# A two-layer streaming encoder step: Toeplitz steps by row halves, a reordered head, q swaps ahead of splits, attention weights in halves

## What is computed

```python
mod = c @ w_ada[layer] + b_ada[layer]                 # the "ada" product
h = rms_norm(x, norm_g[layer]) * (1.0 + scale) + shift
q, k, v, g_a, u, g_s = jnp.split(h @ w_in_even[e], EVEN_SPLITS, axis=-1)
q, k = rope(q), rope(k)
m = jnp.maximum(jnp.max(s, axis=-1, keepdims=True), sink)
p = jnp.exp(s - m)
p = p / (jnp.sum(p, axis=-1, keepdims=True) + jnp.exp(sink - m))
```

## Time and profile before

| what | value |
| --- | --- |
| median of 3 runs | 2287.86 us (2286.92 to 2289.37) |
| the profiled execution's own time | 2290.1 us |
| its span | 2288.3 us |
| mean granted TensorE clock | 0.949 of full |
| TensorE busy | 94% |
| VectorE, ScalarE, GpSimd busy | 36%, 22%, 20% |
| data moved by DMA | 414.93 MB, 181 GB/s on average |

### The profile page before, as it was taken

The page is one execution under the profiler, slowest core; times in us unless marked ns, Lnnn a source line. Parts: engine busy times, 40 slices in busy tenths (PEclk is TensorE's granted clock), DMA queues, the critical chain, the costliest instruction groups (busy, mean ns, idle before and its releaser), DMA issues.

```text
span 2288.3 us, 26857 instructions
## 1 busy us (share of the span) xinstructions
PE 2153.8 (94%) x10930; PEld 1674.9 (73%) x10946; DVE 815.9 (36%) x1506; ACT 498.9 (22%) x1030; POOL 451.8 (20%) x319
## 2 busy tenths in 40 slices
PE   8886899899999999999999999999998989999996
PEld 2356666688887767888887578887886757788885
DVE  7444262433335543122434522114152442422222
ACT  1132343322321421001214311002112431200010
POOL 0033514455524001101123010101023001100011
PEclk9887999899999999999999999999878989999998
DMA  8876744688787425554585245554733313344431
GB/s 279 286 203 230 261 151 173 233 306 295 253 291 245 163 86 177 214 185 166 187 268 172 82 166 212 192 184 155 214 114 108 110 37 111 113 146 148 147 131 59
DMA packets 86271, 414.93 MB, mean 181 GB/s; under 512 B 12404, under 2 KB 13460, under 8 KB 51892
## 3 DMA queue, kind: packets, MB, share of 16 engines
q1 hardware_dynamic: 79360, 396.37, 49.5%
q10 hardware_dynamic: 6788, 16.84, 2.6%
HBM read 323.51 MB, written 86.33 MB: 179 GB/s over the span
## 4 chain that ended last, share of the span: by engine, by line
PE 88%; DVE 4%; DMA 2%; issue 1%; POOL 1%; ACT 1%; SPq 0%; DVEq 0%; ACTq 0%; POOLq 0%
PE bank L699 21%; PE bank L700 21%; PE bank L701 21%; PE bank L954 5%; PE bank L644 3%; PE bank L720 2%; PE bank L719 2%; PE bank L913 1%; PE bank L832 1%; PE bank L914 1%; PE bank L790 1%; PE bank L894 1%; PE bank L820 1%; PE bank L763 1%; DMA parts_scratch<-pair 1%
## 5 line engine op out<-in xcount | busy, mean ns | idle before, releaser
L699 PE MATMUL bank<-p_hh,pair 128*128 128x512 f32 x1952 | 785.3, 402 | 28.0 <-POOL pair L464 14.7
L700 PE MATMUL bank<-p_hl,pair 128*128 128x512 f32 x1952 | 775.9, 398 | 0.0
L701 PE MATMUL bank<-p_hh,pair 128*128 128x512 f32 x1952 | 773.1, 396 | 0.0
L699 PEld LDWEIGHTS bank<-p_hh,pair 128*128 128x128 f32 x1952 | 372.9, 191 | 128.3 <-POOL pair L464 16.1
L701 PEld LDWEIGHTS bank<-p_hh,pair 128*128 128x128 f32 x1952 | 372.5, 191 | 83.0
L700 PEld LDWEIGHTS bank<-p_hl,pair 128*128 128x128 f32 x1952 | 373.0, 191 | 80.1 <-issue 1.4
L464 POOL TENSOR_TENSOR pair<-ring,pair 128x1024 fp32r<-128x1024 f32 x62 | 154.8, 2500 | 194.0 <-ACT pair L455 194.0
L1289 POOL TENSOR_TENSOR pp_mem<-pp_mem 128x512 f32<-128x512 f32 x48 | 62.1, 1294 | 619.2 <-ACT pp_mem L1054 619.2
L1378 POOL TENSOR_TENSOR p_g<-p_t,pp_mem 128x512 f32<-128x512 f32 x32 | 41.3, 1290 | 577.3 <-DVE p_t L1834 577.3
L1708 DVE SCALAR_TENSOR_TENSOR p_x<-bank,mod,p_x 128x512 f32<-128x512 f32 x64 | 47.4, 750 | 261.3 <-PE bank L701 261.3
L1808 DVE TENSOR_TENSOR pp_mem<-p_sw,bank 128x512 f32<-128x512 f32 x32 | 22.0, 688 | 309.9 <-PE bank L701 309.7
(11 more groups left out here) (305 smaller groups left out, 2445.0 us busy)
## 6 DMA issues: line engine op xcount, KB each, us to landing
pair<-parts_scratch SPq DMA_DIRECT2D x198, 1024.0 KB, 4.8
parts_scratch<-pair SPq DMA_DIRECT2D x66, 1024.0 KB, 7.5
ring<-in_dense SPq DMA_DIRECT2D x62, 512.0 KB, 5.1
pair<-ssm_scratch SPq DMA_DIRECT2D x24, 1024.0 KB, 7.2
ring<-in_ada SPq DMA_DIRECT2D x24, 512.0 KB, 4.5
p_H<-in_ada SPq DMA_DIRECT2D x24, 512.0 KB, 4.7
p_x<-in_x SPq DMA_DIRECT2D x4, 2048.0 KB, 25.9
pair<-glu_scratch SPq DMA_DIRECT2D x8, 1024.0 KB, 5.5
```

Of the source, the lines that this page charges most:

```text
L699: pe.matmul(o, ah, bh, start=first, stop=False)
L700: pe.matmul(o, ah, bl, start=False, stop=False)
L701: return pe.matmul(o, al, bh, start=False, stop=last)
```

## The change

- `toeplitz_rows(m)` does what two calls did: its 16 matmuls alternate between the row halves and between banks 0 and 1, and it waits for both banks. It runs after ada chunks 28 to 31 in place of 32 to 35; ScalarE's copies and the `cout` store move with it, the store ahead of the copies. The first load of x follows.
- `load_early` of u0 and u1 goes before ada chunk 40, of u2 and u3 before chunk 44.
- The 6 additions of the prompt's first squares go from GpSimd to VectorE.
- u0 to u3 are all split ahead of the first inverse root on GpSimd, and ahead of the copies of ada rows 10 and 11 on ScalarE; k is split right after the first block's `shift`; the copy of ada rows 9 comes after four squares.
- The swaps of q0 and q1 go ahead of the splits of q2 and q3.
- The sinks' exponential and `normalise` are done in two halves of four heads, the counts of `sink_exp`, `den`, `rden` and `normed` are doubled, and `turn_probs` turns the first half's two banks before the second's. ScalarE now copies banks 0 and 2, VectorE 1 and 3.

```diff
--- before.py
+++ after.py
@@ -102,8 +102,8 @@
             "gelu": 8, "y_turned": 4, "tanh_gate": 8, "gate": 8, "glu_parts": 8, "glu_gate": 4, "mixed_s": 4,
-            "row_max": 4 * NT, "neg_max": 4 * NT, "mask_set": 1, "exped": 4 * NT, "sink_in": NT, "sink_exp": NT,
-            "den": NT, "rden": NT, "normed": NT, "pt_act": 2 * NT, "pt_dve": 2 * NT, "mixed_a": NT,
+            "row_max": 4 * NT, "neg_max": 4 * NT, "mask_set": 1, "exped": 4 * NT, "sink_in": NT, "sink_exp": 2 * NT,
+            "den": 2 * NT, "rden": 2 * NT, "normed": 2 * NT, "pt_act": 2 * NT, "pt_dve": 2 * NT, "mixed_a": NT,
             "x1_ready": 8, "x2_ready": 8, "c_copied": 8, "conv_in": 8, "tail_set": 8, "tail_kept": 8,
@@ -141,7 +141,7 @@
         scores = lambda t: [(f"s{t}_{j}", [("exped", 4 * t + j + 1)]) for j in range(4)]
-        turns = lambda t: [(f"pt{t}_{a}", [("pt_act" if a < 2 else "pt_dve", 2 * t + a % 2 + 1)]) for a in range(4)]
+        turns = lambda t: [(f"pt{t}_{a}", [("pt_dve" if a % 2 else "pt_act", 2 * t + a // 2 + 1)]) for a in range(4)]
         sums = lambda l: (f"nc{l}", [(f"mean{l}", 1)])
@@ -384,7 +384,7 @@
-        B_STEPS, C_STEPS = 20, 32
+        B_STEPS, C_STEPS = 20, 28
@@ -514,13 +514,14 @@
                 s = i % NADASLOT
-                if i == 42:
+                if i == 40:
                     sp.wait_ge(dve_built, TOEPLITZ)
                     load_early(range(2))
+                elif i == 44:
+                    load_early(range(2, NEARLY))
                 if i >= NADASLOT:
...
                 sp.dma_start(ada_slots[s], w_ada[i]).then_inc(raw_in[s], 16)
-            load_early(range(2, NEARLY))
             sp.wait_ge(ada_used, NADA)
@@ -665,20 +666,21 @@
-            def toeplitz_rows(n):
-                if n == 0:
+            def toeplitz_rows(m):
+
+                if m == 0:
                     pe.wait_ge(dve_built, C_POWERS)
-                pe.wait_ge(prep_free, 7 + n)
+                pe.wait_ge(prep_free, 8 + 2 * m)
                 for a in range(4):
-
-                    q, gg = 4 * (n // 2) + a, n % 2
-                    rows = slice(HD * gg, HD * gg + HD)
-                    o = psum[n % 2][0:CH, a * P:(a + 1) * P]
-                    pe.matmul(o, powers[rows, q, L - 1, :], cpow[rows, q, 0:L, :].rearrange("p j c -> p (j c)"),
-                              start=True, stop=False)
-                    mm2 = pe.matmul(o, powers_im[rows, q, L - 1, :],
-                                    cpow_im[rows, q, 0:L, :].rearrange("p j c -> p (j c)"), start=False, stop=True)
-                mm2.then_inc(prep_full, 1)
+                    q = 4 * m + a
+                    for c, (w, x) in enumerate(((powers, cpow), (powers_im, cpow_im))):
+                        for gg in range(2):
+                            rows = slice(HD * gg, HD * gg + HD)
+                            mm = pe.matmul(psum[gg][0:CH, a * P:(a + 1) * P], w[rows, q, L - 1, :],
+                                           x[rows, q, 0:L, :].rearrange("p j c -> p (j c)"), start=(c == 0),
+                                           stop=(c == 1))
+                            if a == 3 and c == 1:
+                                mm.then_inc(prep_full, 1)
@@ -687,11 +689,11 @@
                     ada_turn(i // 4 - 1)
-                for n in range(2):
-                    if B_STEPS <= i < B_STEPS + 4:
-                        b_powers(2 * (i - B_STEPS) + n)
-                    elif C_STEPS <= i < C_STEPS + 4:
-                        toeplitz_rows(2 * (i - C_STEPS) + n)
+                if B_STEPS <= i < B_STEPS + 4:
+                    b_powers(2 * (i - B_STEPS))
+                    b_powers(2 * (i - B_STEPS) + 1)
+                elif C_STEPS <= i < C_STEPS + 4:
+                    toeplitz_rows(i - C_STEPS)
@@ -811,9 +813,9 @@
-                S.wait(pe, blk, "normed", t + 1)
                 for a in range(4):
-                    kt, hh = a // 2, a % 2
+                    kt, hh = a % 2, a // 2
+                    S.wait(pe, blk, "normed", 2 * t + hh + 1)
                     rows = P if kt == 0 else S.KW - P
@@ -1010,9 +1012,12 @@
-            for i in range(36):
+            for i in range(C_STEPS + 4):
                 if i % 4 == 3:
                     copy_rows((i // 4,))
+                if i == C_STEPS:
+                    act.wait_ge(dve_built, C_MATRIX)
+                    act.dma_start(scratch[2], cout_stage).then_inc(scratch_out, 16)
                 for n in range(2):
@@ -1030,12 +1035,9 @@
                     act.dma_start(scratch[0], xin_stage).then_inc(scratch_out, 16)
-                elif i == C_STEPS + 1:
-                    act.wait_ge(dve_built, C_MATRIX)
-                    act.dma_start(scratch[2], cout_stage).then_inc(scratch_out, 16)
             act.wait_ge(scratch_out, 32)
             act.dma_start(prompt.g[:, :, :], xs[0][:, :, 0:TB]).then_inc(prompt.sem["x_early"], 16)
-            copy_rows((9,))
+            copy_rows((8,))
@@ -1102,12 +1104,15 @@
                     ins.then_inc(S.sem["exped"], 1)
-                S.wait(act, b, "sink_in", t + 1)
-                act.activation(S.st[0:S.TP, 4, :], S.st[0:S.TP, 3, :], ACT.Exp).then_inc(S.sem["sink_exp"], 1)
+                    if j % 2:
+                        S.wait(act, b, "sink_in", t + 1)
+                        at = slice(2 * j - 2, 2 * j + 2)
+                        act.activation(S.st[0:S.TP, 4, at], S.st[0:S.TP, 3, at], ACT.Exp)\
+                            .then_inc(S.sem["sink_exp"], 1)
...
                 for a in range(2):
-                    o = S.read(act, b, f"pt{t}_{a}")
+                    o = S.read(act, b, f"pt{t}_{2 * a}")
                     if t > 0:
@@ -1125,7 +1130,6 @@
                 hi = lambda name: split_hi(act, blk, name, streams)
-                hi("k")
                 hi("v")
@@ -1143,13 +1147,13 @@
                 hi("q1")
-                for name, i in (("q2", 0), ("q3", 1), ("ga0", None), ("ga1", 2), ("ga2", 3), ("ga3", None)):
-                    for S, b in streams(blk):
-                        if i in (0, 1):
-                            swap(S, b, f"q{i}", 1 + i)
+                for i in range(2):
+                    for S, b in streams(blk):
+                        swap(S, b, f"q{i}", 1 + i)
+                for name, i in (("q2", None), ("q3", None), ("ga0", None), ("ga1", 2), ("ga2", 3), ("ga3", None)):
                     hi(name)
                     for S, b in streams(blk):
-                        if i in (2, 3):
+                        if i:
                             swap(S, b, f"q{i}", 1 + i)
@@ -1248,16 +1252,15 @@
             square(sample, 1, 0)
-            square(prompt, 0, 0, range(3))
-            copy_rows((10,))
-            square(prompt, 0, 0, range(3, KT))
-            for name in ("u0", "u1"):
+            square(prompt, 0, 0, range(4))
+            copy_rows((9,))
+            square(prompt, 0, 0, range(4, KT))
+            for name in ("u0", "u1", "u2", "u3"):
                 split_hi(act, 1, name, streams_of)
-            copy_rows((11,))
+            copy_rows((10, 11))
             act.wait_ge(prep_done, 2)
             shift(prompt, 0, 0)
-            for name in ("u2", "u3"):
-                split_hi(act, 1, name, streams_of)
+            split_hi(act, 1, "k", streams_of)
             shift(sample, 1, 0)
@@ -1305,8 +1308,7 @@
                 lo = lambda name: split_lo(pool, blk, name)
-                for name in ("k", "v"):
-                    lo(name)
+                lo("v")
                 for S, b in streams(blk):
@@ -1387,18 +1389,16 @@
-            for S, b in ((sample, 1), (prompt, 0)):
-                for k in range(KT):
-                    add_squares(S, b, 0, k)
+            for k in range(KT):
+                add_squares(sample, 1, 0, k)
+            for name in ("u0", "u1", "u2", "u3"):
+                split_lo(pool, 1, name)
             for S, b in ((prompt, 0), (sample, 1)):
                 inverse_root(S, b, 0)
-            for name in ("u0", "u1"):
-                split_lo(pool, 1, name)
             pool.wait_ge(ada_used, NADA)
...
             pool.wait_ge(prep_done, 2)
-            for name in ("u2", "u3"):
-                split_lo(pool, 1, name)
+            split_lo(pool, 1, "k")
             for blk in range(1, NBLK + 1):
@@ -1676,20 +1676,23 @@
             def normalise(S, b, t):
-                S.wait(dve, b, "sink_exp", t + 1)
-                dve.tensor_tensor(S.st[0:S.TP, 5, :], S.st[0:S.TP, 2, :], S.st[0:S.TP, 4, :], ALU.add)\
-                    .then_inc(S.sem["den"], 1)
-                S.wait(dve, b, "den", t + 1)
-                dve.reciprocal(S.st[0:S.TP, 6, :], S.st[0:S.TP, 5, :]).then_inc(S.sem["rden"], 1)
-                S.wait(dve, b, "rden", t + 1)
-                dve.tensor_tensor(S.p[0:S.TP, :, :], S.p[0:S.TP, :, :],
-                                  S.st[0:S.TP, 6, :].unsqueeze(2).to_broadcast([S.TP, NH, S.KW]), ALU.mult)\
-                    .then_inc(S.sem["normed"], 1)
+
```

(20 more changed lines are left out.)

## The result

The changed kernel takes 2247.8 us (median of 4 runs, 2246.6 to 2249.3), the kernel before 2287.4 (4 runs beside them, 2286.7 to 2289.4): a ratio of 0.9827, 95% interval 0.9815 to 0.9839. That is 39.6 us, where 25.1 were predicted; 2263 and its range of 2254 to 2275 both lie above the result. The profiled execution's own time is 2246.9 us.

A forecast was written before the change was run, and what follows sets the result against it. TensorE, busy for 94% of the span, was taken as the bound. Gains of 7.4 + 4.7 + 6.1 + 6.9 = 25.1 us off 2290.1 give 2265.0, and with the median 2.2 lower 2263 us; range 2254 to 2275.

The forecast's parts named there:

- head read and first norm: Head: norm sums 7.4 us sooner through earlier Toeplitz and loads, then 4.7 us less from sums to norm_rows.
- q swaps first: Block 1, ahead of xr: swapping before the q2 split shortens the 9.7 us wait to 3.62, gaining 6.1 us.
- weights in halves: Attention in blocks 1 to 4: shorter waits for the weights' multiplication and transposes done meanwhile, 6.9 us in all.
- The Toeplitz step: Head: alternating row halves cuts each pair of calls from 3.17 to 1.85 us, gaining 5.3 us of TensorE work.
- the xr wait: Block 1, ahead of the xr matmuls: the 9.7 us wait becomes 3.62, as in block 2.
- the sums at 118.5: End of the head: the norm sums start at 118.5 us, 7.4 sooner, with the loads as limit.
- a held port: First norm: by the skill's port rule the diagonal would wait for GpSimd's root, so the gain would be 4.5 us.
- (c): Block 1: the head's and swap's gain, 18.2 us, is waited away at a later transfer; 2281 us, chance 0.07.
- (d): Head, 67 us to norm sums: the fallen clock does not come back; slower, 2299 us, chance 0.03.
- (a): Head: loads collide as hard and the clock falls twice, taking 6 of the 7.4 us; 2269 us, chance 0.19.
- (b): Head: no new stall, so 4.6 us more gain; 2258 us, chance 0.09.
- Sum: Whole kernel: adds the gains 7.4, 4.7, 6.1 and 6.9 to 25.1 us, for a forecast of 2263 us.

The follow-up runs named there:

- b_swaps: The kernel before with only the prompt's q0 and q1 swapped ahead of the splits of q2 and q3; 2281.6 us, ratio 0.9971.
- b_d4: The kernel before with the first matmul of block 2's chunk c4 issued four times more; 2289.1 us, ratio 1.0003.
- b_c4: The kernel before with the first matmul of block 3's chunk c4 issued four times more; 2276.4 us, ratio 0.9955.
- b_halves: The kernel before with only the attention weights normalised and turned in halves; 2266.4 us, ratio 0.9898.
- b_pad50: The kernel before with 50 tiny VectorE instructions, each waited for, as a pure delay ahead of block 1; 2298.6 us, ratio 1.0048.
- a_d3: The changed kernel with three repeats of the first matmul of block 2's chunk c4; 2267.2 us, ratio 0.9907 against the kernel before.

## Why the prediction missed

**What held.** The four terms, to 2.6 us, by the two traces and by the parts alone:

| term | predicted | traces | alone |
|---|---|---|---|
| head read and first norm | 7.4 + 4.7 | 7.1 and 12.2 in all | 13.1 |
| q swaps first | 6.1 | 5.6 | 6.1 |
| weights in halves | 6.9 | 9.5 | 21.4, less 13.7 of clock |

The Toeplitz step (1.85 predicted, 1.86), the multiplication of 1024 elements (1.22, 1.23), the xr wait (3.62, 3.61) and the sums at 118.5 (118.8) are nearly exact. The halves gave 3.5 in block 1 (2.5 predicted), 1.9 each in blocks 2 and 3 (1.85), and in block 4 0.9 for the prompt (0.7) and some 1.3 for the sample, where I had nothing. The sums at 118.8 are in part luck. I had 2.8 us of slow clock at 67 and the last chunk's load as the limit. Neither came: the clock stayed full from 66.2 to 81.3 and TensorE did not wait for the last chunks. In their place came two waits earlier on, 3.00 and 1.68, with 1.7 us of low clock behind each. The diagonal started at 122.07 and took 0.69 us although GpSimd was then in the sample's root (122.01 to 122.56), so the 4.5 that the prediction worked out from a held port did not come; from sums to norm_rows the gain was 5.0. Rivals (c) and (d) did not happen. Of (a) the two falls of the clock came, but not its price of 6 us; (b), 2258, lies nearest by its time, but not by its mechanism, for both stalls came.

**What failed** is the step "Sum": 7.4 + 4.7 + 6.1 + 6.9 = 25.1, taken from the time of before as though all work in between kept its length. It left out the clock of stretches that the change doesn't touch. With the traces' 27.3 for the four terms, 12.0 for the v product and 1.7 for the stall the sum is 41.0, against 39.6 of the medians. The kernel before lost these 13.7 us in a place that small shifts can take it out of, and the halves' shift happened to do it. That low clock stood in its windows, at full TensorE load, and I had read only the windows of the head; my one rival on the clock had it as a loss in the head. A low clock with TensorE busy all the time should have been a rival on the fast side, priced at 12 us: 25.1 + 12.0 off the own time of 2290.1, and 2.2 more for the median, gives 2251.

The Trainium skill, "TensorE: Matmul & The Clock Gate", section "Why this matters for your kernels", advises against long idle gaps between bursts of matmuls, so that the clock doesn't drop mid-kernel. The v product of the kernel before shows that this isn't enough: TensorE had been without a gap for over 80 us, and the clock fell. The same page, Part 1, says that the gate's observation is free-running, that is, not started by the kernel. The traces agree: the instants of change lie differently against the first instruction, 0.16 us behind it in one trace and 3.09 in another.

## What to carry to other kernels

Before summing what a change saves, list the stretches in which TensorE is busy without a gap and its granted clock is still 0.50: such a stretch may come or go with a shift ahead of it, in either direction. The low v product did. Not every one does: another low stretch, of 20.5 us from 1680.4 in the kernel before, stands in the changed kernel too (from 1638.7). Small matmuls directly ahead of a long run of 128-column ones are such a place. A single small product moved between 512-column ones kept the full clock here wherever it fell; two in a row did not. And when an edit gives more than its terms, try a few repeated matmuls in its place before crediting the edit: here 12 of them gave 10 us.

## What the runs showed of the hardware

TensorE's clock fell to 1.2 GHz with no idle time before it, while matmuls of 32, 64 and then 128 columns kept it busy, and it stayed there for 22 us of 128-column matmuls until those of 512 columns came (from 1661.4; back at 1663.5). Where the same 128-column matmuls started at 2.4 GHz they stayed at 2.4 GHz to their end: they kept the level that they met. In all 18 traces the v product was wholly one or the other: 48 or 49 matmuls in the 10 us, or 92. Of the 10 runs of b_swaps one took 2267.5 us where the others took 2279.8 to 2286.5, and b_d4 has two such among ten (2276.1, 2278.5 beside 2287.7 to 2294.4): the clock can come out the other way in single executions of one kernel, though mostly it does not. The kernel before does it too: 3 of its 78 runs took 2274.1 to 2278.2, where its median is 2287.

In the profiled execution of the kernel before, the 512-column matmuls of block 3's second layer stood 0.2333 us apart and not 0.2289 as in the changed kernel, 3 us over the layer at a granted clock of 1.00 in both: 430 matmuls recorded in 100 us,

```profile
1400.00:1500.00 100.00, 100.00 (x430) 80.98 (x429) 17.71 (x35) 6.89 (x12) 10.22 (x8) 1.00 0.53 190
```

against 439 in the changed kernel:

```profile
1372.00:1472.00 100.00, 100.00 (x439) 82.05 (x438) 17.72 (x35) 7.48 (x13) 10.19 (x8) 1.00 0.54 189
```

Six of the 18 traces have such a stretch of about 175 us, and not at the same place: b_c4, b_halves, b_pad50 and b_swaps in the second layer of block 2 (430 or 431 matmuls in 100 us, where the kernel before has 438), a_d3 in block 1. So it is worth some 3 us to a single execution, and comes at the full granted clock. With one trace of each kernel it can't be told what decides where it comes, and its cause is open. The execution of the kernel before that has it here took 2.7 us more than the median.
